# Hybrid layers of a 256-token block: heads side by side in the TensorE array, retention values centred first, mask and maximum in one instruction, four first PSUM banks

## The chip, the cores and the metric

The kernel runs on one core of one Trainium2 chip. The metric is the device time of one execution in microseconds (us); lower is better. The engines named here are TensorE (PE, with its weight loads PEld), VectorE (DVE), ScalarE (ACT) and SyncE (SP), which issues the DMAs of the weights.

## What is computed

Two blocks follow each other on 256 tokens of width 1024, all in float32. The first block (feed-forward, a gated linear recurrence, dilated attention) is not touched. The second puts 16 meta tokens in front (272 tokens) and runs two hybrid layers; each is a mixer and a feed-forward part. The change is in the mixer alone:

```python
q_r, k_r, v_r, g_r, u_p, q_f, k_f, v_f, f_logit = split(h @ w_in)
# retention, 4 heads, dk 48, dv 96
scores = einsum('bnihd,bnjhd->bnhij', rotary(q_r), rotary(k_r) * dk**-0.5) * dmask
inner  = einsum('bnhij,bnjhe->bnihe', scores, v_r)          # and the carried state
o_r = silu(g_r) * head_group_norm(o_r, ret_gn_g)            # (o - mean) * rsqrt(var + eps) * g, per head
# pooling, 4 windows
o_p = multiscale_pool(u_p, pool_w, pool_scale)
# forgetting attention, 6 heads of 64
c = cumsum(log_sigmoid(f_logit + b_f))
s = q_f @ k_f.T * d**-0.5 + c[:, None] - c[None, :]         # causal mask, softmax
o_f = softmax(where(mask, s, -1e30)) @ v_f
mix = concat([o_r, o_p, o_f]) @ w_out                       # then residual and layer norm
```

The mean over a head's 96 outputs is linear in the values: with values whose mean over the 96 entries is taken off first, the outputs have mean zero, because the mixing weights of a token are the same for all 96 entries.

## The kernel before, in words

Activations lie feature-major in SBUF: 8 tiles of 128 features by 272 (or 256) tokens. Every weight matrix comes in chunks of 128 output columns. A chunk is loaded by SP into one of four `raw` slots; ACT rounds it to fp32r (`whi`, L1047) and DVE subtracts to get the rest (`wlo`, L1522). PE multiplies with three fp32r products per 128x128 tile (L490 to L492), so that a chunk of the mixer's input projection is 24 matmuls of 272 columns. PE's work on a chunk is called a tile s here; ACT then copies its accumulator (L1384, semaphore `acc_free`) to where it is used.

`hybrid(l)` exists once for each engine, with a loop over the 22 tiles `s` of `MIX_ORDER` (gate 0, four for rotary q and k, three retention values, then keys, queries and values of the attention, two for the pool, three gates). What stands under `if s == n` is an order written out by hand: on PE it comes behind tile n, on ACT between the rounding of chunk s + 2 and the copy of tile s, on DVE behind the rest of chunk s + 2. Each engine's queue is in order, so what waits holds up all behind it. The two first tiles run together (`first_chunks`), as the features of x arrive.

Around the tiles lie the small products, in plain fp32, each of which appears as two matmul records: `ret_scores` (L881, two calls of two heads, each head in its own 32 rows of the array), `ret_values` (L853), `ret_means` (L896, all-ones by the outputs), `ret_variance` (L906), `ret_spread` (L913, the reciprocal deviation to all rows), `fox_scores` (per head: q by k over 64 rows, L830, and the cumulated logits over 12 rows by fp32r, L833, three token tiles), `fox_transposed` (L846), `fox_values` (L853, one head) and `pool_products` (L922). Tiles alternate between banks 0 and 1 (`two_banks`), so tile s waits until ACT has copied tile s - 2. All `fox_scores` use banks 2 and 3, and head h waits until DVE has read head h - 1.

On ACT, tile 0 is copied behind three instructions on the forget logits (L1366 to L1368, with a table load). On DVE stand the logarithm of the forget gates in eight parts (`cumulative_logits`), `rotate` (L1952 to L1954), `decay` (L1986), `centre` (L1994), `mask_max` (mask L1922, maximum L1927, three token tiles each), `normalise` (L1934, L1938) and the pool. Behind the tiles, PE begins the two first chunks of the output projection (`begin`, in `BEGIN_ORDER`) as their inputs become ready.

Of the kernel before, what the change touches and what calls it, by code (L numbers as in the profile page):

```python
# [73 lines left out]
BEGIN_ORDER = (6, 4, 5, 7, 0, 1, 2)  # L74
# [15 lines left out]
B_SEL = B_EXP + RET_HEADS * P  # L90
# [6 lines left out]
B_HEAD = B_CNT + 2 * TOK  # L97
B_LO = B_HEAD + RET_HEADS * RET_HEADS
# [32 lines left out]
def build(nc, x_in, meta_in, par_in, con_in, bias_in, con2_in, poolw_in, weights, out):  # L131
# [89 lines left out]
    rden_f = place("rden_f", [2, 3])  # L221
    assert cursor[0] <= hhi_at
# [106 lines left out]
    fx_done = sem("fx_done")  # L329
    fe_done = sem("fe_done")  # L330
# [4 lines left out]
    rot_done = sem("rot_done")  # L335
    up_zero = sem("up_zero")
# [8 lines left out]
    ret_mean = sem("ret_mean")  # L345
    ret_xc = sem("ret_xc")
# [72 lines left out]
    spread_bank = (6, 7, 6, 7)  # L419
# [66 lines left out]
    def _(pe):  # L486
# [310 lines left out]
        def hybrid(l):  # L797
# [15 lines left out]
            def fox_scores(h):  # L813

                rows = slice(HD * (h % 2), HD * (h % 2 + 1))
                pe.wait_ge(acc_free, mix_evicted(st, "q", h // 2))
                if h == 0:
                    pe.wait_ge(c_done, l + 1)
                    pe.wait_ge(sel_done, l + 1)
                    pe.wait_ge(vt2_copied, 2 * l + 1)  # L820
                if h == 2:

                    pe.wait_ge(vt2_copied, 2 * l + 2)
                if h:
                    pe.wait_ge(biased, HEADS + f0 + h)
                b = 2
                for q, (bank, c) in enumerate(((b, 0), (b, FOX_AT[1]), (b + 1, 0))):
                    n = FOX_COLS[q]
                    o = ps[0:QT[q], bank, c:c + n]
                    nc.tensor.matmul(o, qf[rows, h // 2, token_tiles(q)], kf[rows, h // 2, 0:n], start=True, stop=False)  # L830

                    parts = slice(LOGIT_ROW, LOGIT_ROW + LOGIT_ROWS)
                    last = nc.tensor.matmul(o, sel_r[parts, h * P:h * P + QT[q]], c_parts[parts, 0:n], start=False, stop=True)  # L833
                last.then_inc(scored, 1)

            def fox_transposed(h):
                pe.wait_ge(probs_ready, HEADS + f0 + h + 1)
                if h == 0:

                    pe.wait_ge(ret_xc, RET_HEADS * l + 1)  # L840
# [16 lines left out]
            def fox_values(h):  # L857
                o = ps[HD * (h % 2):HD * (h % 2 + 1), 5, :]
                pe.wait_ge(vt2_copied, 2 * l + 2)
                pe.wait_ge(pT_copied, HEADS + f0 + h + 1)  # L860

                pe.wait_ge(at_ready, PAIRS + 3 * l + h // 2)
                by_values(o, vf_tok, slice(HD * h, HD * (h + 1)), pT_fox[:, h % 2, :]).then_inc(pv_done, 1)
# [8 lines left out]
            def ret_scores(pair):  # L872

                if pair[0] == 0:
                    pe.wait_ge(rot_done, 4 * (l + 1))
                for k in range(3):
                    for half in range(2):
                        for h in pair:
                            rows = slice(32 * h, 32 * h + 32)
                            o = ps[0:QT[k], score_bank[h], KEY_AT[k]:KEY_AT[k] + KEY_COLS[k]]  # L880
# [5 lines left out]
            def ret_values(h):  # L886
                pe.wait_ge(vt2_copied, 2 * l + 1)
# [5 lines left out]
            def ret_means(h):  # L893

                pe.wait_ge(ret_osb, RET_HEADS * l + h + 1)
                nc.tensor.matmul(ps[0:RET_DV, out_bank[h], 0:TOK], ones_head[0:RET_DV, 0:RET_DV], osb[0:RET_DV, h, :],  # L896
                                 start=True, stop=True).then_inc(ret_mean, 1)

            def ret_variance(h):

# [25 lines left out]
            for s in range(WIN_TILES):  # L926
# [21 lines left out]
                if s == 12:  # L948
                    fox_scores(1)
# [1327 lines left out]
```

## Time and profile before

| | before |
|---|---|
| median of 3 runs | 1849.24 us (1844.86 to 1849.54) |
| profiled execution, its own time | 1849.01 us |
| its span in the profile | 1847.2 us |
| busy PE, PEld | 1801.1 us, 1623.2 us |
| busy DVE, ACT | 1298.9 us, 980.4 us |
| chain that ended last | PE 92%, DVE 5%, ACT 2% |

The spans of the engines overlap. A line of the profile names the source line (L), the engine, the operation, the tiles written and read, shapes and times. The PE spans of neighbouring matmuls overlap too, since they are pipelined: what one costs is the step to the next one's start. Layer 0 of the mixer (`mix0`) starts near 1128 us, layer 1 (`mix1`) near 1495 us.

### The profile page before, as it was taken

The numbers are of one execution on the slowest core, as the hardware profiler recorded it, in microseconds if no ns is written. First come the engines' busy times: TensorE is split into PE (matmuls) and PEld (weight loads), VectorE is DVE, ScalarE is ACT, GpSimd is POOL, SyncE is SP. The second block draws the span as 40 slices with busy tenths as digits, with TensorE's granted clock in tenths as the row PEclk, the third lists the DMA queues.
The fourth block names the chain that finished last, engine by engine and source line by source line (L and its number), as shares of the span: only waits on it lengthen the run. The fifth ranks groups of instructions, "written<-read, shape, count | busy, mean of one in ns | idle before, by whom it ended". The sixth has DMA issues, their size and how long they took to land.

```text
span 1847.2 us, 33301 instructions
## 1 busy us (share of the span) xinstructions
PE 1801.1 (98%) x11784; PEld 1623.2 (88%) x11784; DVE 1298.9 (70%) x2113; ACT 980.4 (53%) x1712; POOL 0.2 (0%) x4
## 2 busy tenths in 40 slices
PE   8999998999999999999899997999999989999998
PEld 7888998888898888888788887879999988788887
DVE  6776889777656776688877667568656575687765
ACT  5564695655456563555565545354434354556553
POOL 0000000000000000000000000000000000000000
PEclk9999999999999999999899998999999999999999
DMA  6565364556545565333455651323556433245562
GB/s 225 186 204 190 126 191 153 171 188 219 167 144 176 189 207 176 107 103 104 167 172 192 214 170 51 106 96 106 171 170 205 159 104 103 89 136 185 183 210 86
DMA packets 76637, 290.97 MB, mean 158 GB/s; under 512 B 9344, under 2 KB 11648, under 8 KB 76544
## 3 DMA queue, kind: packets, MB, share of 16 engines
q1 hardware_dynamic: 76544, 289.70, 48.2%
q8 instruction: 62, 1.02, 0.2%
q14 instruction: 31, 0.25, 0.0%
HBM read 288.62 MB, written 1.05 MB: 157 GB/s over the span
## 4 chain that ended last, share of the span: by engine, by line
PE 92%; DVE 5%; ACT 2%; issue 1%; DMA 0%; SPq 0%; ACTq 0%; DVEq 0%
PE psum L498 32%; PE psum L499 16%; PE psum L490 12%; PE psum L492 11%; PE psum L491 11%; PE psum L853 1%; PE psum L736 1%; PE psum L630 1%; DVE r L1694 1%; DVE wlo L1522 1%; PE psum L830 1%; PE psum L625 1%; PE psum L735 1%; PE psum L846 1%; PE psum L833 0%
## 5 line engine op out<-in xcount | busy, mean ns | idle before, releaser
L1522 DVE TENSOR_TENSOR wlo<-raw,whi 128x1024 fp32r<-128x1024 f32 (+3 forms) x496 | 644.7, 1309 | 268.6 <-ACT whi L1047 267.9
L498 PE MATMUL psum<-x_split,whi 128*128 128x512 f32 x1760 | 618.5, 395 | 6.4 <-DVE x_split L1557 3.8
L1047 ACT ACTIVATE whi<-raw 128x1024 fp32r<-128x1024 f32 (+3 forms) x496 | 548.8, 1119 | 39.0 <-PE psum L492 20.4
L499 PE MATMUL psum<-x_split,wlo 128*128 128x256 f32 x1760 | 494.2, 281 | 0.0
L498 PEld LDWEIGHTS psum<-x_split,whi 128*128 128x128 f32 x1760 | 331.0, 188 | 85.2 <-issue 3.9
L490 PE MATMUL psum<-x_split,whi 128*128 128x272 f32 (+1 forms) x1184 | 351.2, 297 | 13.7 <-ACT gsb L1384 7.7
L492 PE MATMUL psum<-x_split,wlo 128*128 128x272 f32 (+1 forms) x1184 | 342.1, 289 | 0.0
L491 PE MATMUL psum<-x_split,whi 128*128 128x272 f32 (+1 forms) x1184 | 341.5, 288 | 0.0
L499 PEld LDWEIGHTS psum<-x_split,wlo 128*128 128x128 f32 x1760 | 331.4, 188 | 0.0
L498 PE MATMUL psum<-h_split,whi 128*128 128x512 f32 x770 | 272.2, 397 | 0.0
L490 PEld LDWEIGHTS psum<-x_split,whi 128*128 128x128 f32 x1184 | 227.3, 192 | 22.5 <-ACT gsb L1384 8.2
L491 PEld LDWEIGHTS psum<-x_split,whi 128*128 128x128 f32 x1184 | 227.4, 192 | 0.2
L492 PEld LDWEIGHTS psum<-x_split,wlo 128*128 128x128 f32 x1184 | 227.2, 192 | 0.0
L499 PE MATMUL psum<-h_split,wlo 128*128 128x256 f32 x770 | 216.2, 281 | 0.0
L1115 ACT ACTIVATE small<-psum 128x256 f32<-128x256 f32 x220 | 84.4, 383 | 223.8 <-PE psum L499 223.6
L490 PE MATMUL psum<-h_split,whi 128*128 128x256 f32 (+3 forms) x614 | 178.2, 290 | 4.9 <-DVE wlo L1522 2.5
L492 PE MATMUL psum<-h_split,wlo 128*128 128x256 f32 (+3 forms) x614 | 175.4, 286 | 0.0
L491 PE MATMUL psum<-h_split,whi 128*128 128x256 f32 (+3 forms) x614 | 175.2, 285 | 0.0
L498 PEld LDWEIGHTS psum<-h_split,whi 128*128 128x128 f32 x770 | 144.7, 188 | 34.1
L1150 ACT ACTIVATE sq<-r 128x256 f32<-128x256 f32 (+2 forms) x70 | 29.4, 420 | 227.9 <-DVE r L1671 227.9
L499 PEld LDWEIGHTS psum<-h_split,wlo 128*128 128x128 f32 x770 | 145.6, 189 | 0.1
L1596 DVE TENSOR_TENSOR whole<-psum,small 128x256 f32<-128x256 f32 x220 | 93.1, 423 | 62.9 <-ACT small L1115 62.9
(229 smaller groups left out, 1820.8 us busy)
## 6 DMA issues: line engine op xcount, KB each, us to landing
raw<-w_in SPq DMA_DIRECT2D x264, 512.0 KB, 3.4
raw<-w_out SPq DMA_DIRECT2D x96, 704.0 KB, 4.1
raw<-w_mix SPq DMA_DIRECT2D x44, 512.0 KB, 3.4
raw<-w_rg SPq DMA_DIRECT2D x25, 512.0 KB, 3.8
raw<-w_q SPq DMA_DIRECT2D x24, 512.0 KB, 3.5
raw<-w_mixo SPq DMA_DIRECT2D x16, 576.0 KB, 3.7
raw<-w_kv SPq DMA_DIRECT2D x16, 512.0 KB, 4.3
raw<-w_rg_out SPq DMA_DIRECT2D x8, 640.0 KB, 3.9
```

The costliest lines, as they stand in the source:

```text
L490: nc.tensor.matmul(acc(bank, T), whi[slot][0:rows, w], hi, start=start, stop=False)
L491: nc.tensor.matmul(acc(bank, T), whi[slot][0:rows, w], lo, start=False, stop=False)
L492: return nc.tensor.matmul(acc(bank, T), wlo[slot][0:rows, w], hi, start=False, stop=stop)
L498: nc.tensor.matmul(ps[:, bank, :], whi[slot][:, w], split, start=start, stop=False)
L499: return nc.tensor.matmul(part(bank, 0), wlo[slot][:, w], split[:, 0], start=False, stop=stop)
L625: return nc.tensor.matmul(acc(4, T), ones_d, tile[:, t], start=first, stop=last)
L630: ins = nc.tensor.matmul(ps[:, 5, col + m:col + m + 1], tile[:, c:c + P], ones_d[:, 0:1], start=not started, stop=last and m == len(starts ...
L1047: nc.scalar.activation(whi[slot][:, 0:cols], raw[slot][:, 0:cols], ACT.Copy).then_inc(w_hi_done, count)
L1115: nc.scalar.activation(small[:, b, j % 2, :], part(j, 1), ACT.Copy).then_inc(small_out, 1)
L1150: nc.scalar.activation(sq[:, i + j, t], r[:, i + j, t], ACT.Square).then_inc(sq_done, 1)
L1522: V.tensor_tensor(wlo[slot][:, 0:cols], raw[slot][:, 0:cols], f(whi[slot][:, 0:cols]), ALU.subtract).then_inc(w_lo_done, 1)
L1596: ins = V.tensor_tensor(whole[:, b, j % 2, :], part(j, 0), small[:, b, j % 2, :], ALU.add)
```

## The change

1. Tiles 0 to 3 have a bank each (`mix_bank`); tiles 2 and 3 wait for no copy, tiles 4 and 5 for those of tiles 0 and 1 (wait s - 3), later ones as before. The three ACT instructions on the logits move to s = 2 (`forget_logits`) and read the copied gate.
2. `ret_scores` does four heads at once behind tile 6, in banks 4 to 7.
3. The transposed retention values are centred by DVE (`centre_values`: three sums, three scalar_tensor_tensor with a broadcast) as they leave PSUM, in place of three ACT copies. `ret_means` and `centre` are gone. ACT copies and squares each output from PSUM; `ret_values` run together behind tile 10.
4. `ret_variance` puts four heads in four groups of 32 columns of the array, the root and the reciprocal run over 128 rows, and `ret_spread` reads one row, through bank 5, one head behind the other.
5. `fox_scores` and `fox_values` work on pairs of heads: scores on row groups 0 to 63 and 64 to 127 with banks 2, 3 and 6, 7, logits now over 64 rows with zeros (a second copy of `c_parts` and `sel_r` in the other half), values on column groups 0 to 63 and 64 to 127.
6. `mask_max` is one `tensor_tensor_reduce` per token tile: (score + mask) * -1 and its minimum; `exps` scales by -1. `normalise` takes one reciprocal in place of three.
7. The orders on all three engines and `BEGIN_ORDER` are new.

```diff
+BEGIN_ORDER = (6, 7, 4, 5, 0, 1, 2)
+RET_ORDER = (2, 3, 0, 1)
...
+    mix_bank = lambda s: s if s < 4 else s % 2
...
-                    from_x(st, s // SLOTS, s % SLOTS, two_banks(s), st.u0 + s - 1)
+                    from_x(st, s // SLOTS, s % SLOTS, mix_bank(s), st.u0 + max(0, s - (3 if s < 6 else 1)))
...
+                for q in range(3):
+                    for h in heads:
+                        rows = slice(HD * (h % 2), HD * (h % 2 + 1))
+                        nc.tensor.matmul(out(h, q), qf[rows, pair, token_tiles(q)], kf[rows, pair, 0:FOX_COLS[q]],
+                                         start=q != 1, stop=False, skip_group_check=True)
+
+                for q in range(3):
+                    for h in heads:
+                        rows = slice(HD * (h % 2), HD * (h % 2 + 1))
+                        ins = nc.tensor.matmul(out(h, q), sel_r[rows, h * P:h * P + QT[q]], c_parts[rows, 0:FOX_COLS[q]],
+                                               start=False, stop=True, skip_group_check=True)
...
+                for k in range(3):
+                    for h in heads:
+                        e = h % 2
+                        ins = nc.tensor.matmul(ps[HD * e:HD * (e + 1), 5, QT_AT[k]:TOK], vf_tok[0:QT[k], k, HD * h:HD * (h + 1)],
...
+                for h in range(RET_HEADS):
+                    ins = nc.tensor.matmul(ps[32 * h:32 * h + 32, 5, 0:TOK], ones_head[0:RET_DV, 0:32], sqh[0:RET_DV, h, :],
+                                           start=True, stop=True, skip_group_check=True)
...
             for s in range(WIN_TILES):
                 tile(s)
                 if s == 6:
+                    ret_scores()
...
                 if s == 10:
+                    for h in RET_ORDER:
+                        ret_values(h)
+                if s == 11:
                     fox_scores(0)
                 if s == 12:
+                    ret_variance()
+                if s == 13:
...
+                    transposes(vf, 3, ((2, 0), (3, 0), (4, 0))).then_inc(vt2_done, 1)
+                if s == 14:
+                    ret_spread(0)
+                if s == 15:
+                    fox_transposed(0)
                     fox_scores(1)
...
+                if s == 2:
+                    forget_logits()
...
+                if s == 13:
+                    act.wait_ge(ret_var, l + 1)
+                    nc.scalar.activation(std4[:, :], ps[:, 5, 0:TOK], ACT.Sqrt, bias=eps[:, 0:1]).then_inc(ret_std, 1)
                     exps(0)
...
+                    ins = V.tensor_tensor_reduce(s_fox[0:m, h % 3, c:c + n], ps[0:m, at[0], at[1]:at[1] + n],
+                                                 con2[0:m, B_MASK + c:B_MASK + c + n], -1.0, 3e38, ALU.add, ALU.min,
+                                                 nmax_f[0:m, b, q:q + 1])
...
                 if s == 2:
+                    V.memset(f(c_parts[:, :]), 0.0)
+                    V.memset(den_f[:, :, :], 1.0).then_inc(den_one, 1)
                     cumulative_logits(0)
...
                 if s == 14:
+                    dve.wait_ge(ret_std, l + 1)
+                    V.reciprocal(std4[:, :], std4[:, :]).then_inc(ret_rstd, 1)
+                    normalise(0)
```

On DVE, s = 3 to 8 stay as they were: `rotate(0)` and part 1 of the logits at s = 3, parts 2 and 3 at 4, `rotate(1)` at 5, parts 4 and 5 at 6, `decay` at 7 and 8.

## Rows read from the trace of the kernel before

**Rows 1.** The page's first part: busy time of the engines over the span.
```profile
PE 1801.1 (98%) x11784; PEld 1623.2 (88%) x11784; DVE 1298.9 (70%) x2113; ACT 980.4 (53%) x1712; POOL 0.2 (0%) x4
```
**Rows 2.** Timeline of PE: start, us, instruction, idle before it; starts of both layers.
```profile
1138.24 0.59 PE L490 MATMUL psum<-x_split,whi 128*128 128x272 f32 x1 [3.87 <-ACT gsb L1384]
...
1158.32 0.39 PE L490 MATMUL psum<-x_split,whi 128*128 128x272 f32 x1
...
1506.46 0.60 PE L490 MATMUL psum<-x_split,whi 128*128 128x272 f32 x1 [3.88 <-ACT gsb L1384]
...
1525.22 0.39 PE L490 MATMUL psum<-x_split,whi 128*128 128x272 f32 x1
```
**Rows 3.** Timeline of ACT in that wait of layer 0.
```profile
1134.10 1.06 ACT L1047 ACTIVATE whi<-raw 128x1024 fp32r<-128x1024 f32 x1 [1.41 <-PE psum L492]
...
1136.05 1.28 ACT L1368 ACT_TABLE_LOAD   x1
1137.35 0.42 ACT L1368 ACTIVATE sgate<-sgate 12x272 f32<-12x272 f32 x1
```
**Rows 4.** Busy time by stretch: PE, PEld, DVE, ACT, POOL, PEclk, DMA, GB/s.
```profile
1138.22:1141.61 3.39, 3.37 (x15) 3.37 (x16) 2.24 (x3) 3.39 (x7) 0.00 (x0) 0.50 0.29 114
...
1137.59:1144.41 6.82, 6.17 (x27) 6.17 (x28) 3.37 (x3) 4.30 (x11) 0.00 (x0) 0.50 0.49 151
...
1574.49:1577.91 3.42, 3.42 (x16) 3.42 (x16) 3.30 (x7) 0.00 (x0) 0.00 (x0) 0.50 0.52 172
280.84:287.67 6.83, 4.36 (x21) 4.10 (x20) 6.52 (x9) 2.35 (x3) 0.00 (x0) 0.50 0.27 89
```
**Rows 5.** Timeline of PE in the recurrence stage, ahead of the last stretch of rows 4.
```profile
279.58 0.36 PE L490 MATMUL psum<-h_split,whi 128*128 128x256 f32 x1 [2.04 <-DVE h_split L1784]
```
**Rows 6.** The chain of waits in order of time, layer 0: start, us, what.
```profile
1156.37 2.02 PE psum L881 x24
...
1161.61 2.02 PE psum L881 x24
...
1178.58 1.09 PE psum L896 x4
...
1181.65 0.27 PE psum L833
...
1196.08 1.93 PE psum L906 x8
...
1213.88 1.13 PE psum L853 x6
```
**Rows 7.** PE's groups by shape: count, busy us, mean ns of one, both layers.
```profile
L881 PE MATMUL psum<-rot 32*112 32x272 f32 x32 | 4.7, 410 | 0.0
...
L896 PE MATMUL psum<-osb,con 96*96 96x272 f32 x16 | 4.5, 402 | 0.0
```
**Rows 8.** Timeline of DVE in layer 0, tiles 2 to 6.
```profile
1140.56 0.30 DVE L1540 TENSOR_SCALAR prod<-sgate 12x272 f32<-12x272 f32 x1
...
1144.59 0.44 DVE L1952 TENSOR_TENSOR rtmp<-rot_in,con 128x272 f32<-128x272 f32 x1 [1.85 <-ACT rot_in L1384]
...
1148.78 1.23 DVE L1522 TENSOR_TENSOR wlo<-raw,whi 128x1024 fp32r<-128x1024 f32 x1 [0.33 <-ACT whi L1047]
...
1155.68 1.22 DVE L1522 TENSOR_TENSOR wlo<-raw,whi 128x1024 fp32r<-128x1024 f32 x1
```
**Rows 9.** DVE's groups by shape: count, busy us, mean ns of one.
```profile
L1922 DVE TENSOR_TENSOR s_fox<-psum,con 64x272 f32<-64x272 f32 x12 | 5.1, 423 | 0.0
L1927 DVE TENSOR_REDUCE nmax_f<-s_fox 64x1 f32<-64x272 f32 x12 | 5.0, 418 | 0.0
...
L1541 DVE RECIPROCAL prod<-prod 12x272 f32<-12x272 f32 x2 | 3.7, 1848 | 0.1
```
**Rows 10.** Timeline of ACT around the root of the variance, layer 0.
```profile
1204.71 1.28 ACT L1452 ACT_TABLE_LOAD   x1
```
**Rows 11.** Busy time of the stretch in which ACT does one head's exponentials.
```profile
1216.57:1218.01 1.44, 1.44 (x9) 0.95 (x8) 0.71 (x3) 1.44 (x6) 0.00 (x0) 1.00 0.23 42
```

More of the change, by code:

```diff
@@ L221, in build @@
     rden_f = place("rden_f", [2, 3])
+    v_sum = place("v_sum", [3, RET_HEADS])
     assert cursor[0] <= hhi_at
@@ L806, in tile, with fox_scores @@
                 if s >= FIRST:
-                    from_x(st, s // SLOTS, s % SLOTS, two_banks(s), st.u0 + s - 1)
+                    from_x(st, s // SLOTS, s % SLOTS, mix_bank(s), st.u0 + max(0, s - (3 if s < 6 else 1)))
             def token_tiles(t):
                 return slice(QT_AT[t], QT_AT[t] + QT[t])
[L813 to L817, printed above, removed]
+            def fox_scores(pair):
+                heads = (2 * pair, 2 * pair + 1)
+                pe.wait_ge(acc_free, mix_evicted(st, "q", pair))
+                if pair == 0:
@@ L818, in fox_scores @@
                     pe.wait_ge(c_done, l + 1)
                     pe.wait_ge(sel_done, l + 1)
[L820 to L833, printed above, removed]
@@ L834, in fox_scores, with out @@
-                last.then_inc(scored, 1)
+                    pe.wait_ge(vr_centred, l + 1)
+                    pe.wait_ge(ret_sq, RET_HEADS * l + 2)
+                if pair == 1:
+                    pe.wait_ge(vt2_copied, l + 1)
+                if pair:
+                    pe.wait_ge(biased, HEADS + f0 + 2 * pair)
+                def out(h, q):
+                    bank = (2 if h % 2 == 0 else 6) + q // 2
+                    c = FOX_AT[1] if q == 1 else 0
+                    return ps[0:QT[q], bank, c:c + FOX_COLS[q]]
@@ L1479, in hybrid @@
             copy_transposed(5)
+            act.wait_ge(pool_mm, l + 1)
+            for m in range(2):
+                nc.scalar.activation(h_hi[:, RET_HEADS + m, :], acc(2 + m, TOK), ACT.Copy,
+                                     scale=par[:, C_PS + 2 * l + m:C_PS + 2 * l + m + 1]).then_inc(pool_hi, 1)
             next_chunk(by_name[f"mixo{l}"], 0, 0)
@@ L1932, in normalise @@
                 dve.wait_ge(probs, HEADS + f0 + h + 1)
-                for q in range(3):
-                    ins = V.reciprocal(rden_f[0:QT[q], b, q:q + 1], den_f[0:QT[q], b, q:q + 1])
-                link(ins)
+                link(V.reciprocal(rden_f[:, b, :], den_f[:, b, :]))
                 for q, (c, n, m) in enumerate(zip(FOX_AT, FOX_COLS, QT)):
@@ L1990, in hybrid, with centre_values @@
             hd = slice(0, RET_DV)
-            def centre(h):
-                dve.wait_ge(ret_mean, RET_HEADS * l + h + 1)
-                V.tensor_tensor(osb[hd, h, :], osb[hd, h, :], ps[hd, out_bank[h], 0:TOK], ALU.subtract).then_inc(ret_xc, 1)
+            def centre_values():
+                dve.wait_ge(vt2_done, 2 * l + 1)
+                by_head = lambda tile: tile.rearrange("p (h d) -> p h d", h=RET_HEADS)
+                for t in range(3):
+                    ins = V.tensor_reduce(v_sum[0:QT[t], t, :], by_head(ps[0:QT[t], 2 + t, 0:FOX_W]), AX.X, ALU.add, negate=True)
+                link(ins)
+                for t in range(3):
+                    n = QT[t]
+                    less = v_sum[0:n, t, :].unsqueeze(2).broadcast_to([n, RET_HEADS, RET_DV])
+                    ins = V.scalar_tensor_tensor(by_head(vr_tok[0:n, t, :]), less, 1.0 / RET_DV, by_head(ps[0:n, 2 + t, 0:FOX_W]),
+                                                 ALU.mult, ALU.add)
+                ins.then_inc(vr_centred, 1)
             def norm_output(h):
```

252 lines of the change are left out of this document (95 added, 157 removed).

## The prediction

> **What bounds the kernel now.** I read the page's first part, then the idle time of PE, then the granted clock by stretch, then the order of DVE and ACT where PE will arrive earlier. PE is busy for 98% of the span [rows 1], so time goes only where PE has fewer steps, waits less, or runs at the higher clock. In the two mixer stages three things are seen. First, PE stands still for 3.87 and 3.88 us when tile 2 wants bank 0 [rows 2]: ACT has the rounding of a chunk, two instructions on the logits, a table load of 1.28 us and an exponential ahead of the copy [rows 3]. Second, the granted clock is at 0.50 (1.2 GHz in place of 2.4) in five stretches of the two stages, of which rows 4 show the first, 6.82 us, and the last, 3.42 us; the first covers that wait, the last follows a run of small products. A stretch of 3.42 us that is full of work costs half of itself, 1.7 us. Third, a tile of 24 matmuls takes 3.2 us (from the end of one L881 group at 1158.39 to the next at 1161.61 [rows 6]), while the small products of a head cost up to 2.3 us.
>
> **Fewer steps on PE, for one layer.**
> - Scores of the retention: two calls of 2.02 us [rows 6] become one. Two heads in different row groups already run together: 32 matmuls of 272 columns keep PE busy for 4.7 us, where 16 with one head at a time need 4.5 us [rows 7]. I take 2.2 us for four heads; if only two overlap it stays at 4.0. Gain 1.8 (0 to 2.0).
> - Means: four matmul pairs, 1.09 us for two of them [rows 6]. Gain 2.0 (the second two start under the tail of a tile).
> - Scores of the attention: a head takes 2.25 us (from 1179.67, the end of L896, to 1181.92, the end of the last L833 [rows 6]), six heads 13.5 us. For a pair, q by k is two passes over 592 columns. The L881 group does two halves by two passes over 496 columns in 2.02 us, 1.02 ns per column and step; this gives 1.2 us for both heads together. The logits are one pass of 592 columns; a tile of 3.2 us for 24 times 272 columns is 0.49 ns per column, so 0.3 us together, 0.6 us one by one. With 0.3 us for filling the array twice it is 1.8 us, and 5.4 for three pairs. Gain 8.1. The worst end, no overlap at all, is 3.9 us a pair: gain 1.8.
> - Variance: 1.93 us [rows 6] for eight records, one head at a time. Four column groups of which each runs alone would stay there; together they are two steps of 0.27 and a fill, 0.75 us. Gain 1.2 (0 to 1.3).
> - Values of the attention: 1.13 us a head [rows 6], 6.8 us. No row shows two column groups at once. The nearest rows are the row groups of rows 7, which overlap fully; I take 1.2 us a pair, 3.6 us, gain 3.2, with 0 as the other end.
> - Spread: four single pairs in place of two double ones, 0.65 each against 0.54. Loss 0.4.
> - Transposes, retention values and pool stay.
>
> The sum is 1.8 + 2.0 + 8.1 + 1.2 + 3.2 - 0.4 = 15.9 us for a layer.
>
> On the column groups, the Trainium skill speaks in two ways. TensorE: Matmul & The Clock Gate, Part 3, has three column groups at 2.38 times the speed of one; by that a pair costs about 1.4 us and the sum loses 0.7 us. The same part says that weight loads go under running matmuls only where the row groups differ, and both heads of a pair use all rows here; by that nothing overlaps among columns (a rival below). In this trace loads do run under matmuls that use the same rows, since PE and PEld are busy for 98% and 88% of one span [rows 1].
>
> **The wait at tile 2, and what is late next.** Four banks take the 3.87 us away. PE then asks for tile 6 early, and tile 6 needs the rest of its chunk, which DVE does behind `cumulative_logits(0)`, `rotate(0)` and part 1. The first of them waits for the exponential of the logits. In the new order ACT does more ahead of that: a second rounding, five scaled copies of x and two tile copies. A stretch of 3.39 us holds one such rounding, five copies of x and one tile copy [rows 4]; with 0.3 for the other copy it is 3.7 us. Before, the exponential ended 3.67 us after the start at 1134.10 [rows 3], so now it ends 7.35 us after it. From there DVE needs 6.0 us to the rest of chunk 6 (1140.56 to 1148.78, less 1.85 and 0.33 idle [rows 8]), and 6.9 us more to the end of `rotate(1)` (1148.78 to 1155.68). So chunk 6 is ready 1.2 us later, 14.7 us after the start, where PE would be at 12.5 (four tiles of 3.13 and nothing else): a wait of 2.2 us. The rotation ends at 20.3 us; PE, with tile 6 done at 17.9, waits 2.4 us more. Four scores then take until 22.4 us. Tile 7 started 24.2 us after 1134.10 in layer 0 (1158.32), and in layer 1, counted from the same place before its wait, 22.9 us. The gain of the start is thus 1.8 us and 0.5 us, not 3.9 plus the clock: DVE's chain takes it over. Of the 15.9 us, 1.8 for the scores lie behind the second call at tile 7, which is simply gone (2.0), and the longer first call is counted here; the tail keeps 2.0 + 2.0 + 8.1 + 1.2 + 3.2 - 0.4 = 16.1.
>
> **A new wait at the first spread.** It stands behind tile 14 and needs the reciprocal of the deviation. On ACT, after the rounding behind tile 12: table load 1.28 [rows 10], root 0.4, table load 1.28 again for `exps(0)` of 1.44 [rows 11], a copy 0.3, a rounding 0.95, 5.6 us; ahead of these 1.5 us for a copy and a rounding; on DVE then the rest 1.1 and the reciprocal 1.85 [rows 9]. That is 10.1 us from the end of tile 12. PE needs 0.75 + 3.13 + 1.0 (transposes) + 3.13 = 8.0. A wait of 2.1 us, behind which tile 15 is queued. At the very end I find 0.8 us for the third pair's output, which is needed last. Centring, six instructions of some 0.5 us on DVE, hides beside tile 9 and 10; without cover it would cost up to 1.5 us. The tail's gain is 16.1 - 2.1 - 0.8 = 13.2 us per layer.
>
> **Mask and maximum.** Two instructions of 423 and 418 ns [rows 9] become one. It is no operation that the trace shows. One pass like the mask is the low end (1.1 us a head with three tiles), the sum of both the middle (1.8), the reciprocal, 1848 ns for 272 columns, the dearest row. I take 1.1 to 1.3; up to 1.8 costs nothing, since DVE has room in the tail. `normalise`, the memsets and the wider root and `sel_r` go with it at nothing, under PE's tiles.
>
> **Clock.** Two stretches in layer 0's tail and one in layer 1's go, 1.7 us each, if nothing takes their place. But a wait of 2.04 us [rows 5] in another stage was followed by 6.83 us at 0.50 [rows 4], and three waits of 2.1 to 2.4 us per layer are new. I charge one stretch of 3.4 us (1.7) at the start and one behind the spread for each layer, and one more for the two together: 8.5 us. Low end 0; high end 6.83 at each place, 17 us.
>
> **Sum.** Start 1.8 + 0.5, tails 26.4, old stretches 5.1, new ones -8.5: 25.3 us. From the profiled execution, 1849.0 us (0.2 below the median of the runs), this gives 1823.7, and I say 1824. Its own range is 1816 to 1832.
>
> **Rivals.**
> - Column groups, or heads with shared queues, don't overlap. Columns alone cost 2.5 us a layer (values back, of which the last wait swallows some), 1829; with no overlap for the attention's scores either, 2 x 8.7 us, 1841. For: the rule above. Against: rows 7. Chance 0.12, at 1829 to 1843.
> - The waits are longer, and each opens 6.83 us at half clock: some 12 us more, 1836. For: rows 4 and 5. Against: in the start DVE's chain decides anyway, so slow PE work there is half hidden. 0.14.
> - Slower: the new instruction costs as much as the reciprocal and some of a second pass, 2.0 us each, 6 us a head. DVE would then have 36 us of it beside some 25 us of other work from tile 12 on, where PE needs 50: laid out along the queues, the wait at the spread grows, since mask 1 stands ahead of the reciprocal, and each pair of scores waits for masks. At 4.0 us a head a layer loses 6 us, at 6 about 18: 1859. It decides from 5.1 us a head (1.7 us each). For: the operation is unseen. Against: no two-input row of that shape costs over 0.5 us. 0.06.
> - The change doesn't do what it says, because queues in order give back all of it: each of three waits doubles and no clock returns, 1845. 0.05.
> - Better: the waits stay under what lowers the clock, 1812 to 1816. 0.05.
>
> **Chances and range.** The forecast has 0.58. A run of this kernel can tell 0.3%, 5.5 us, from no change. Faster by more than that: 0.58 + 0.12 + 0.14 + 0.05 = 0.89; within: 0.05; slower: 0.06. The range that leaves out no more than 2 in 10 is 1815 to 1840.
>
> **What would show it.** L881 with 48 records in about 2.2 us; the score pair in 1.8; value pairs in 1.2; no wait of PE at tile 2, but some 2 us each at tile 6, ahead of L881 and at the first spread; mask and minimum near 0.45 us each. Wrong it would be if pairs start a full step apart, or if the clock is at 0.50 for more than 20 us of the two stages.

## The result and the profile after

The changed kernel takes 1826.01 us (median of four runs, 1824.91 to 1826.48), the kernel before 1847.62 us in the same series (1844.86 to 1849.54). The ratio is 0.9887 with a 95% interval of 0.9872 to 0.9902: 21.6 us faster. The profiled execution took 1825.73 us, its span is 1824.0 us, against 1849.0 and 1847.2 before. Forecast were 1824 and a gain of 25.3 us. One of the four executions of the kernel with the start in another order (below) took 6010.63 us and stands in no other number here.

In the changed kernel the lines have moved: L903 are the retention scores (L881 before), L839 and L845 the products and logits of the attention scores (with L833), L882 the attention values (L853), L919 the variance (L906), L927 the spread, L860 the transposes, L1906 mask and maximum (L1922 and L1927).

TensorE (PE) is as full as it was [rows 1], busy for 28.8 us less:

```profile
PE 1772.3 (97%) x11768; PEld 1607.0 (88%) x11768; DVE 1290.3 (71%) x2099; ACT 977.8 (54%) x1706; POOL 0.2 (0%) x4
```

The chain of waits of layer 0, in order of time: start, us, what. It shows how long each packed group is, in place of those of rows 6.

```profile
1153.95 2.12 PE psum L903 x48
...
1177.24 1.34 PE psum L839 x12
1178.58 0.49 PE psum L845 x6
...
1202.02 0.62 PE psum L927 x2
...
1216.22 1.14 PE psum L882 x12
```

Four retention heads take what two took in rows 6. A pair's attention scores take 1.34 + 0.49 us, where one head took 2.25. A pair's values take 1.14 us, where one head took 1.13 us. The variance, in the timeline of PE, has gone from 1.93 us to 0.67 (0.60 to the start of what follows):

```profile
1182.22 0.67 PE L919 MATMUL psum<-sqh,con 96*32 96x272 f32 x8
```

PE's waits, by line and releaser, first in the stretch of layer 0's mixer (from 1120 to 1260 us):

```profile
PE psum L492 <- DVE wlo L1505: 2.5, 1, 2.5
PE psum L927 <- DVE std L2044: 2.4, 1, 2.4
PE psum L588 <- DVE r L1654: 1.0, 1, 1.0
PE psum L903 <- DVE rot L1935: 0.8, 1, 0.8
PE psum L492 <- DVE h_split L1925: 0.8, 1, 0.8
```

Then in that of layer 1 (from 1465 to 1612 us), where the first two and the scores have the same lengths:

```profile
...
PE psum L588 <- DVE r L1654: 1.1, 1, 1.1
...
PE psum L492 <- DVE h_split L1925: 1.0, 1, 1.0
```

The wait for bank 0 at tile 2, 3.87 us in rows 2, is gone. In its place stand five waits, all for DVE: 2.46 us at tile 6, 0.80 ahead of the scores, 2.42 at the first spread, 0.79 and 1.01 at the end of the stage (0.75, 1.00 and 1.06 for the second, fourth and fifth in layer 1). They sum to 7.5 us in layer 0 and 7.7 in layer 1; the old wait was 3.9 in each.

The granted clock is at 0.50 (1.2 GHz) in these stretches among others; the columns are those of rows 4:

```profile
1148.32:1151.73 3.41, 3.32 (x15) 3.35 (x16) 3.27 (x7) 0.00 (x0) 0.00 (x0) 0.50 0.49 154
1192.69:1199.52 6.83, 6.83 (x28) 5.93 (x27) 3.08 (x10) 0.56 (x2) 0.00 (x0) 0.50 0.38 128
1595.46:1602.29 6.83, 6.63 (x29) 6.48 (x30) 4.12 (x9) 1.89 (x3) 0.00 (x0) 0.50 0.53 160
1547.68:1551.09 3.41, 3.41 (x17) 3.41 (x17) 2.22 (x7) 0.00 (x0) 0.00 (x0) 0.50 0.42 126
```

Each of the four begins between 0.2 us before and 1.0 us behind the end of a wait: of tile 6 at 1148.41, of the spread at 1192.53 and 1546.65, of the last one in layer 1 at 1595.66. A fifth, 3.41 us from 1503.30, stands at tile 6 of layer 1. PE is nearly full in them (busy for 3.32 to 3.41 of 3.41 us, 6.63 and 6.83 of 6.83), and a stretch costs half of its length where nothing else is waited for. The five sum to 23.9 us; in the kernel before the five of the same stages were 20.5.

By place the gain of 23.2 us in the span is, measured in PE's timeline from one sum over a row of ones (L627, L625 before) to the next (L588, L586 before): 144.3 to 131.4 us in layer 0, a gain of 12.9; 132.9 to 120.9 us in layer 1, 12.0; from there to the following sum 21.4 to 24.4 us, a loss of 3.0, in which the stretch at 1595.46 us lies; and 1.3 us in places that the change doesn't touch.

VectorE's (DVE's) groups by shape in layer 0's mixer (from 1130 to 1250 us), with count, busy us and mean ns, show the operation that no row of before held. It reads its result out in a second record:

```profile
L1906 DVE CUSTOM_DVE_ANT_0 s_fox<-psum,con 64x272 f32<-64x272 f32 x6 | 2.6, 428 | 0.0
L1906 DVE CUSTOM_DVE_ANT_0 s_fox<-psum,con 96x208 f32<-96x208 f32 x6 | 2.2, 364 | 0.0
...
L1906 DVE CUSTOM_DVE_ANT_0 s_fox<-psum,con 112x112 f32<-112x112 f32 x6 | 1.6, 262 | 0.0
...
L1906 DVE DVE_READ_ACCUMULATOR2_ANT nmax_f<- 112x1 f32 x6 | 0.5, 79 | 0.0
```

One pass costs what the mask alone cost [rows 9], and the read 0.08 us.

### The profile page after: what moved, and what is told of

It reads as the page before. It is cut to its first block, busy times and chain, and to the rows that moved or that the text cites. A ratio compares the mean times of both kernels' runs of the same rounds, so it can differ in the third digit from the quotient of the medians.

```text
span 1824.0 us, 33247 instructions
## 1 busy us (share of the span) xinstructions
PE 1772.3 (97%) x11768; PEld 1607.0 (88%) x11768; DVE 1290.3 (71%) x2099; ACT 977.8 (54%) x1706; POOL 0.2 (0%) x4
## 3 DMA queue, kind: packets, MB, share of 16 engines
q1 hardware_dynamic: 76544, 289.50, 50.2%
## 4 chain that ended last, share of the span: by engine, by line
PE 88%; DVE 7%; ACT 3%; issue 1%; DMA 0%; SPq 0%; ACTq 0%; DVEq 0%
PE psum L500 32%; PE psum L501 16%; PE psum L492 11%; PE psum L494 10%; PE psum L493 10%; DVE wlo L1505 2%; PE psum L738 1%; PE psum L632 1%; PE psum L627 1%; DVE r L1677 1%; PE psum L579 1%; PE psum L737 1%; ACT whi L1043 1%; PE psum L860 1%; PE psum L867 1%
## 5 line engine op out<-in xcount | busy, mean ns | idle before, releaser
L1043 ACT ACTIVATE whi<-raw 128x1024 fp32r<-128x1024 f32 (+3 forms) x496 | 548.8, 1119 | 43.0 <-PE psum L494 24.4
```

Source lines behind the costliest of these rows:

```text
L1043: nc.scalar.activation(whi[slot][:, 0:cols], raw[slot][:, 0:cols], ACT.Copy).then_inc(w_hi_done, count)
```

## The experiments

The kernel before was timed beside each series (1847.6, 1845.3, 1846.7 and 1846.6 us), so kernels of different series are compared by their ratios; one thousandth is 1.85 us. By the intervals of two ratios their difference is uncertain by some 4 us. The changed kernel stands at 0.9887.

**The four banks by themselves.** The kernel before, with the bank and waits of the change and with the exponential of the forget gate moved out of the first tile's copy:

```diff
+    mix_bank = lambda s: s if s < 4 else s % 2
...
-                    from_x(st, s // SLOTS, s % SLOTS, two_banks(s), st.u0 + s - 1)
+                    from_x(st, s // SLOTS, s % SLOTS, mix_bank(s), st.u0 + max(0, s - (3 if s < 6 else 1)))
...
+                if s == 2:
+                    forget_logits()
```

> The kernel before with the four first banks and the moved logits alone (part 1 of the change). Theory: DVE's chain takes the start over, because the exponential of the logits comes 3.7 us later: PE stands still about 2.2 us ahead of tile 6 and up to 2.4 us ahead of the first L881 group, and tile 7 starts only 1 to 2 us earlier in each layer; about 1845 us, 2 to 4 us under the kernel before. Rival: what is gained at tile 2 stays, 3.9 us of waiting and 1.7 to 3.4 us of half clock in each layer, 12 us under the kernel before, about 1836 us.

It took 1849.15 us, ratio 1.0021 (1.0008 to 1.0034): no gain, rather a loss of 4 us, not even the 2 to 4 us of the theory. PE's timeline shows why, start, us, idle before it:

```profile
1146.93 0.57 PE L491 MATMUL psum<-x_split,whi 128*128 128x272 f32 x1 [2.46 <-DVE wlo L1526]
...
1152.46 0.48 PE L882 MATMUL psum<-rot 32*112 32x272 f32 x2 [0.81 <-DVE rot L1958]
```

3.27 us of waits replace 3.87. In the profiled execution (1845.2 us, the second shortest of ten that lie from 1844.9 to 1855.7), layer 0 gains 1.6 us and layer 1 loses 1.0, the latter with three stretches of 3.41 us at half clock in the place of two. The rival, in which the whole wait and its clock are gained, falls. DVE's chain takes over, as the prediction said, and alone the banks are worth nothing that can be measured.

**The same products with the heads outermost.** The changed kernel, in which a head's pieces follow one another in the queue instead of alternating with those of the other head; products and places in the array are the same (the loops are those of the scores' products, of the logits and of the values):

```diff
-                for q in range(3):
-                    for h in heads:
+                for h in heads:
+                    for q in range(3):
...
-                for q in range(3):
-                    for h in heads:
+                for h in heads:
+                    for q in range(3):
...
-                for k in range(3):
-                    for h in heads:
+                for h in heads:
+                    for k in range(3):
```

> The changed kernel with the loop over the two heads put outside the loop over token tiles in fox_scores and fox_values; same matmuls, same tiles of the array, same banks. Theory: two heads overlap only when their matmuls stand next to each other in PE's queue; a pair of scores then takes 3.3 to 3.9 us in place of 1.83, a pair of values 2.2 in place of 1.15, together 7 to 9 us a layer, about 1840 to 1844 us. Rival: each group of rows or columns has its own order and overlap does not hang on neighbours: groups stay at 1.8 and 1.15 us, 1826 us.

1837.13 us, ratio 0.9946 (0.9930 to 0.9963), 10.9 us above the changed kernel by the ratios. PE's timeline, first of the changed kernel, then of this one:

```profile
1177.17 1.41 PE L839 MATMUL psum<-kf,qf 64*112 64x112 f32 x12
1178.51 0.56 PE L845 MATMUL psum<-c_parts,sel_r 64*112 64x112 f32 x6
...
1216.15 1.21 PE L882 MATMUL psum<-pT_fox,vf_tok 112*64 112x272 f32 x12
```

```profile
1177.54 2.72 PE L839 MATMUL psum<-kf,qf 64*112 64x112 f32 x12
1180.19 0.56 PE L845 MATMUL psum<-c_parts,sel_r 64*112 64x112 f32 x6
...
1220.44 2.33 PE L882 MATMUL psum<-pT_fox,vf_tok 112*64 112x272 f32 x12
```

The 12 records of a score pair and of a value pair take twice as long: these products are plain fp32, two records each, and now six records of one head stand in a row. For them the overlap hangs on the neighbour in the queue. The logits' 6 records don't move, although their loops are turned as well: these products are fp32r, one record each, with three of one head in a row. In both kernels they start in three pairs, one record of each head (4 ns apart in the changed kernel, 10 ns in this one), and take 0.49 and 0.50 us to the next start. So a neighbour in the queue is not needed for every kind of product; whether the kind or the number of records in a row decides, no run here tells.

From start to next start the score pair goes from 1.34 to 2.65 us and the value pair from 1.15 to 2.26. Three pairs of each in two layers are 14.5 us. The expected 14 to 18 came out as 11: the stretches at half clock sum to 50.2 us in place of 59.8, worth 4.8 us, while all waits of PE sum to 46.7 us against 45.3. The waits for the third pair's output (0.79 and 1.00 us) are swallowed, but those ahead of the retention scores are 1.7 us longer in the two layers.

**Mask and maximum as two instructions.** The changed kernel with the addition and the maximum apart again:

```diff
-                    ins = V.tensor_tensor_reduce(s_fox[0:m, h % 3, c:c + n], ps[0:m, at[0], at[1]:at[1] + n],
-                                                 con2[0:m, B_MASK + c:B_MASK + c + n], -1.0, 3e38, ALU.add, ALU.min,
-                                                 nmax_f[0:m, b, q:q + 1])
+                    ins = V.tensor_tensor(s_fox[0:m, h % 3, c:c + n], ps[0:m, at[0], at[1]:at[1] + n],
+                                          con2[0:m, B_MASK + c:B_MASK + c + n], ALU.add)
...
+                    ins = V.tensor_reduce(nmax_f[0:m, b, q:q + 1], s_fox[0:m, h % 3, c:c + n], AX.X, ALU.max, negate=True)
```

On ACT the scale of -1 of the exponentials goes with it.

> The changed kernel with mask and maximum as two instructions per token tile again. Theory: DVE gets 0.9 us more per head, 10.6 us in all, and PE's waits stay as they are since DVE has room there; within 1.5 us of 1826. Rival: the one instruction was what made room for the pairs; each pair of scores waits about 0.9 us, 4 to 6 us more, 1831 us.

The single run took 1832.4 us, 6.4 above the changed kernel, which by its number speaks for the rival. Its profile does not: the only new wait is 0.36 us in each layer, ahead of the first transposes of the third pair. PE's waits over 0.06 us sum to 49.3 us against 45.3, and only 0.7 of that are the masks: 3.0 stand ahead of the retention scores, 1.5 in each layer, where tile 6 ran at full clock and its half-clock stretch came behind the scores instead (told below). Three kernels below that keep the one instruction show the same in layer 0 (2.28 us ahead of the scores): the reciprocal first, the end in another order, the wait filled. Stretches at 0.50 sum to 66.6 us against 59.8, 3.4 us of time. That run alone couldn't settle it, so the question was put again where those are absent, below.

**The reciprocal first.** The changed kernel with DVE's reciprocal of the deviation ahead of the rest of chunk 16, which stands at s = 14:

```diff
+                if s == 14:
+                    dve.wait_ge(ret_std, l + 1)
+                    V.reciprocal(std4[:, :], std4[:, :]).then_inc(ret_rstd, 1)
                 rest(s)
...
                 if s == 14:
-                    dve.wait_ge(ret_std, l + 1)
-                    V.reciprocal(std4[:, :], std4[:, :]).then_inc(ret_rstd, 1)
                     normalise(0)
```

> The changed kernel with DVE's reciprocal of the deviation ahead of the rest of chunk 16 in its queue, nothing else. Theory: the wait of 2.4 us at the first spread is an order in DVE's queue (the reciprocal stands behind a chunk that ACT rounds only after the exponentials); it goes, and with it the stretch at half clock that follows (3.3 us in layer 0, 1.6 in layer 1): 8 to 10 us under the changed kernel, about 1817 us. Rival: the chunk's rest is late in its place and tile 16 or the first transpose waits; gain under 3 us, over 1823 us.

1816.92 us, ratio 0.9838 (0.9821 to 0.9854), as the theory had it. In the changed kernel DVE's timeline has

```profile
1189.49 1.23 DVE L1505 TENSOR_TENSOR wlo<-raw,whi 128x1024 fp32r<-128x1024 f32 x1 [3.72 <-ACT whi L1043]
1190.63 1.85 DVE L2044 RECIPROCAL std<-std 128x272 f32<-128x272 f32 x1
```

which shows DVE idle for 3.72 us, waiting for a rounding by ACT, then the rest of that chunk, then the reciprocal that PE stands for; ACT had ended the root by 1185.5 us, before most of that idle time. With the reciprocal first no wait is left at the spread in either layer, and neither of the two stretches at 0.50 behind it. The start of this trace has another thing to show: tile 6 at full clock, and a longer wait behind it.

```profile
1149.27 0.36 PE L492 MATMUL psum<-x_split,whi 128*128 128x272 f32 x1 [2.46 <-DVE wlo L1505]
...
1154.81 0.50 PE L903 MATMUL psum<-rot 32*112 32x272 f32 x4 [2.28 <-DVE rot L1935]
```

From tile 6 to the scores it is 5.54 us here, and 5.54 us in the changed kernel (1148.41 to 1153.95), where tile 6 ran at half clock and the wait was 0.80. DVE's chain decides, and a slow clock under it costs nothing.

**The start in another order.** The changed kernel with the forget gate's exponential one step earlier on ACT, ahead of the rounding at s = 1; on DVE the first part of the logits ahead of the rest at s = 1, the second rotation at s = 4 in place of 5, and the other parts of the logits behind both rotations:

```diff
-                round_ahead(st, s // SLOTS, s % SLOTS)
-                if s == 2:
+                if s == 1:
                     forget_logits()
+                round_ahead(st, s // SLOTS, s % SLOTS)
...
+                if s == 1:
+                    cumulative_logits(0)
                 rest(s)
...
                 if s == 3:
                     rotate(0)
+                if s == 4:
+                    rotate(1)
+                if s == 5:
                     cumulative_logits(1)
-                if s == 4:
+                if s == 6:
                     cumulative_logits(2)
                     cumulative_logits(3)
-                if s == 5:
-                    rotate(1)
...
```

> The changed kernel (1826.0) with VectorE's and ScalarE's work at the start of the layer in another order: the exponential of the forget logits ahead of the second tile's rounding, the sum of the logits ahead of the second tile's rest, the two rotations one tile earlier each, and the other sums after them. Nothing is added or left out. Theory (VectorE's chain, not the banks, sets the start now): the waits of 2.46 us at tile 6 and 0.80 and 0.75 us ahead of the retention scores shrink to under 0.5 us together, and so does the half-clock stretch of 3.41 us behind each (about 1 to 1.7 us lost in each): 2 x (2.9 + 1.3) = 8.4 us, 1817 to 1820. Rival (as with the four banks, something else is late next, ScalarE's gate or the wait for the running maximum's buffers): under 2 us gained, 1824 to 1826. Against both: the wait at the first spread (2.42 us) stays as it is in either case.

1811.38 us (1811.26 to 1814.10), ratio 0.9819 (0.9801 to 0.9837): 12.6 us below the changed kernel by the ratios, more than the 8.4 expected. Both waits of the start are gone in both layers. The three longest waits of PE in layer 1 are now

```profile
PE psum L927 <- DVE std L2045: 2.4, 1, 2.4
PE psum L588 <- DVE r L1654: 1.1, 1, 1.1
PE psum L492 <- DVE h_split L1925: 1.0, 1, 1.0
```

All waits of PE over 0.06 us, summed over the span, fall from 45.3 to 40.2 us; the stretches at 0.50 from 59.8 to 39.3, worth half of it, 10.3 us. The two give 15.3 us for a span that is 14.5 us shorter. More of the clock has come back than the stretches at the start: those at 510.0, 1267.78 and 1622.77 us are gone too and the one behind the first spread is halved, while two in other stages have doubled. The stretch that followed the last wait of layer 1 is gone as well, although that wait and the one before it stand there as before:

```profile
1583.00:1590.00 7.00, 6.17 (x50) 6.15 (x51) 5.94 (x13) 3.12 (x6) 0.00 (x0) 1.00 0.58 180
```

So those two waits by themselves don't lower the clock; the reading that tied the stretch at 1595.46 us to them alone is wrong.

**The end in another order.** The changed kernel with the third pair's output ahead of the rest of the first output tile, and the second tile's rest behind the first sum:

```diff
-            rest_of_chunk(*ahead(by_name[f"mixo{l}"], 0, 0))
             rest_of_output(2)
-            rest_of_chunk(*ahead(by_name[f"mixo{l}"], 0, 1))
-            add_to_ax(by_name[f"mixo{l}"])
+            rest_of_chunk(*ahead(by_name[f"mixo{l}"], 0, 0))
+            add_to_ax(by_name[f"mixo{l}"], ahead(by_name[f"mixo{l}"], 0, 1))
```

> The changed kernel with VectorE's order at the end of the stage turned: the third pair's output is split ahead of the first output tile's rest instead of behind it, and the second tile's rest comes behind the first sum. Theory (the two waits at the end, 0.79 and 1.00, 1.01 and 1.06 us, are one queue on VectorE, and the 6.83 us half-clock stretch at 1595.46 us hangs on them): both waits go in both layers, 3.9 us, and with them up to 3.4 us of clock: 1819 to 1823. Rival (the work is only moved: the first output tile's rest is then late for its own reader, and the wait turns up at the row of ones or at the next output tile): 1825 to 1828, with the waits' sum within 1 us of 3.9.

1821.21 us, ratio 0.9864 (0.9849 to 0.9879), 4.2 us below the changed kernel by the ratios. The time is in the theory's range, the waits say half of each: the first of the two is gone in both layers, the second stays, as the rival had it.

```profile
1242.45 0.47 PE L588 MATMUL psum<-r,con 128*128 128x272 f32 x1 [0.80 <-DVE r L1654]
...
1594.37 0.45 PE L588 MATMUL psum<-r,con 128*128 128x256 f32 x1 [1.06 <-DVE r L1654]
```

PE comes to L588 earlier by what it no longer waits, and DVE still has a rest of 1.35 us and a memset of 0.51 us ahead of the sum. The waits that are gone are 1.8 us, and in layer 0 the wait ahead of the scores is 1.5 us longer, at full clock of tile 6. Most of the gain is the clock: the stretches at 0.50 sum to 52.5 us against 59.8, and the 6.83 us at the end of layer 1 are gone although the wait of 1.06 us stands.

**The wait filled.** The changed kernel with four fp32 products that nobody reads ahead of the first spread (of 272 columns each, not of 112 as the expectation says):

```diff
+            def fill_wait():
+                pe.wait_ge(ret_std, l + 1)
+                for _ in range(4):
+                    nc.tensor.matmul(ps[:, 5, 0:TOK], ident, qf[:, 0, :], start=True, stop=True)
...
                 if s == 14:
+                    fill_wait()
                     ret_spread(0)
```

> The changed kernel with four fp32 matmuls of 112 columns that nobody reads put on TensorE between the end of the square root and the first spread, so that TensorE is at work in the part of the wait that remains; the reciprocal is still 1.85 us behind VectorE's other work, and the spread can't start earlier. Theory (the half-clock stretch of 6.83 and 3.41 us behind the wait of 2.42 us is TensorE's idleness, a cost of its own beside the wait): the wait plus filling stays at 2.4 us, the half-clock stretches at 1192.69 and 1547.68 us go: 3.4 + 1.7 = 5.1 us less, 1820 to 1822. Rival (the half-clock stretches are not tied to this wait): they stay or turn up elsewhere, 1825 to 1828.

1820.25 us, ratio 0.9860 (0.9845 to 0.9875). DVE releases the spread as late as before, and PE is at work or idle for 2.57 us ahead of it, against 2.42 idle. But the clock stays up behind it, and the kernel is 5.0 us shorter by the ratios:

```profile
1190.92 2.00 PE L926 MATMUL psum<-qf,con 128*128 128x272 f32 x8
...
1193.49 0.69 PE L932 MATMUL psum<-std,con 1*96 1x272 f32 x2 [0.58 <-DVE std L2050]
...
1193.60:1200.00 6.40, 6.40 (x51) 4.85 (x52) 4.33 (x11) 2.41 (x6) 0.00 (x0) 1.00 0.38 132
```

The third line is the busy time of the stretch behind it: 51 records in 6.4 us at 1.00, where the changed kernel had 28 in 6.83 us at 0.50. The same holds in layer 1. The two stretches behind the spreads were 10.2 us, 5.1 us of time. This is the clock's price apart from the wait's: the idleness of PE, not the spread's lateness, costs it. That the measured 5.0 us equal this price is in part chance, since the profile has more changes: stretches of another 8.4 us less outside the spreads, the 6.83 us at the end of layer 1 among them, and against that a wait ahead of layer 0's scores that is 1.5 us longer, and the filling itself.

**All three orders.** The edits of the reciprocal, the start and the end together.

> The changed kernel with the three orders of VectorE together: reciprocal first (as in e4, which measured 1816.9), the start as in e5, the end as in e6. Theory (the three waits are separate and each brings its own stretch of half clock): the gains add, 9 + 8 + 5 = 22 us, 1802 to 1808. Rival (the half-clock stretches are not removed but fall elsewhere, and only the waits' own 2 x (2.4 + 3.3 + 1.9) = 15 us add): 1811 to 1814.

1800.56 us (1798.5 to 1801.7), ratio 0.9751 (0.9737 to 0.9764), 25.1 us below the changed kernel and just under the expected 1802 to 1808; the three alone give 9.1 + 12.6 + 4.2 = 25.9. The gains add. In the stretch of layer 0's mixer one wait of the five is left, in layer 1 the same one:

```profile
PE psum L588 <- DVE r L1654: 0.8, 1, 0.8
```

All waits over 0.06 us sum to 30.0 us (45.3 in the changed kernel), the stretches at 0.50 to 39.6 (59.8): 15.3 + 10.1 = 25.4 us, and the span is 25.2 us shorter. This kernel is faster than the kernel before and than the changed one.

**Two banks under the three orders.** The last kernel with tiles in two banks from the first on:

```diff
-    mix_bank = lambda s: s if s < 4 else s % 2
+    mix_bank = lambda s: s % 2
...
-                    from_x(st, s // SLOTS, s % SLOTS, mix_bank(s), st.u0 + max(0, s - (3 if s < 6 else 1)))
+                    from_x(st, s // SLOTS, s % SLOTS, mix_bank(s), st.u0 + max(0, s - 1))
```

> The kernel with all three orders (1800.6) with only two first banks, as in the kernel before: tile 2 waits until the first tile is copied out, tile 3 until the second. Theory (the four banks do work once VectorE's chain is out of the way): in the trace with four banks ScalarE ends its copy of the first tile at 1134.2 us and of the second at 1139.1 us, and TensorE would want tile 3 at about 1138.1: a wait of about 1 us at tile 3 in each layer and, as the running chain is fed later, up to 1 us more of clock in each: 1802.5 to 1805. Rival (the banks were never the matter, only the order of the forget gate's exponential was): under 0.5 us in each layer, 1800 to 1801.5. A third: the whole old wait of 3.87 us comes back, with its clock, 2 x 5 us: 1811.

1807.28 us, ratio 0.9789 (0.9772 to 0.9805): 7.0 us dearer than with four banks, and above the expected 1802.5 to 1805. The rival without any effect falls, and so does the one with the whole old wait; the theory's mechanism is there, with a second wait that it had not counted, at tile 2, since ACT ends its copy at 1133.8 us only:

```profile
1133.84 0.39 PE L492 MATMUL psum<-x_split,whi 128*128 128x272 f32 x1 [1.12 <-ACT gsb L1374]
...
1138.73 0.39 PE L492 MATMUL psum<-x_split,whi 128*128 128x272 f32 x1 [1.61 <-ACT rot_in L1374]
```

2.7 us in each layer are 5.4 of the 7.0. The banks that were worth nothing by themselves are worth this once the order on ACT and DVE lets PE use them.

**Two mask instructions under the three orders.** The kernel with all three orders and the edit of the two masks.

> The kernel with all three orders (1800.6) with mask and maximum in two instructions again. In the run of the changed kernel with two instructions the time was 1832.4 (one run), 6.4 above, of which the waits at the third transposes explain 0.37 us in each layer and the half-clock stretches 3.4 us. Theory (one instruction spares VectorE 1 us or so a head, and little of it lies on the path): one wait of 0.4 us in each layer, 0.7 us in all, and up to 2 us of clock: 1801 to 1803.5. Rival (the fused instruction carries more of the gain than its own wait shows): the 6 us again, 1806 to 1808.

1801.68 us, ratio 0.9755 (0.9739 to 0.9771): 0.7 us by the ratios, 1.1 by the medians, no more than can be told from nothing. The wait is the one seen before, in each layer:

```profile
PE psum L860 <- DVE s_fox L1922: 0.4, 1, 0.4
```

So of the 6.4 us of the open run the fused instruction has 0.7 us of waits and 1 us or so of time. The rest goes, by that run's profile, with where the half clock fell, which no repetition of it tests.

## Why the prediction was right, step by step

The kernel came out 2 us above the forecast, inside its range; the mechanism held, and the sizes of several terms did not. That the sum came so near is in part luck, as told at the clock and the waits. No run takes back the four-head scores, the variance or the centring alone: their shares are read from the trace.

- **Fewer steps on PE.** Forecast 15.9 us a layer, measured 16.4: retention scores 2.05 us for the one call (forecast 2.2), score pair 1.83 (1.8: its products 1.34 against 1.2, its logits 0.49 against 0.3, and 0.3 forecast for filling the array), variance 0.60 to the next start (0.75), value pair 1.15 (1.2), spread 0.62 each (0.65); the means' 2.0 us are gone. The value pair was the unseen one. The experiment with the heads outermost gives 2.26 us for the same two heads, so the overlap in column groups is worth a factor of 1.97. It also shows a condition of the fp32 pairs that the prediction took for granted: the order in the queue. Its price, 14.5 us of products and 10.9 us of time, would have been half of the gain.
- **The rival of the column groups** falls. The Trainium skill's TensorE: Matmul & The Clock Gate, Part 3, gives three column groups 2.38 times one and says that weight loads overlap running matmuls only across row groups. Here two column groups that use the same rows reach 1.97 of 2 with a load for each product, so the rule does not decide the time of such pairs, and the measurement goes before it.
- **The start.** Forecast was that DVE's chain takes the four banks' gain over, with a wait of 2.2 us at tile 6 and 2.4 ahead of the scores. Measured 2.46, and 2.28 where tile 6 runs at full clock (0.80 where it doesn't, 5.54 us for both together either way). The gain of the start was forecast at 1.8 and 0.5 us; counted from the stage's first product to tile 7 in layer 0 it is 2.0 (30.4 to 28.4 us), and from the sum over the row of ones before in layer 1 it is 0.8 (36.2 to 35.4), of which 0.4 is a shorter wait at the head of the stage (1.03 to 0.67 us). The kernel with the four banks alone confirms it, and the new order of the start shows what stood behind the chain: 12.6 us.
- **The wait at the spread.** Forecast 2.1 us, measured 2.42 in both layers.
- **The centring** hid, as forecast: six instructions of 0.54 to 0.56 us on DVE, and PE waits for nothing between the scores and the first spread.
- **The end of the stage** is the term that was mis-sized. Forecast was one wait of 0.8 us. Measured are two, 0.79 + 1.01 and 1.00 + 1.06 us. The second, at the row of ones that takes the first sum, was not foreseen: DVE's queue there (the split, a rest of 1.34, a memset of 0.51, the sum) was not laid out past the third output. It costs 2.1 us in the two layers.
- **The clock.** The charge of 8.5 us came out right in sum and wrong in its terms. Of it 3.4 stood for the starts; stretches of 3.41 us did come there, and cost nothing, since the wait behind them shrank by as much. Behind the spreads were 6.83 and 3.41 us (5.1 us, charged 3.4), and at the end of layer 1 6.83 us (3.4, charged 1.7 for the two layers). 8.5 again, by other ways; that the sums agree is luck. Together with the two at the starts the clock was at 0.50 for 23.9 us of the two stages. The prediction had called more than 20 us a sign that it was wrong, and on the clock this sign came. The old stretches, 5.1 us in the tails, are indeed gone, but 3.41 us from 1622.77 and others outside the two stages came up.
- **Sum.** 2 x 16.4 us less work, less 2 x 3.7 us of more waiting, is 25.4 us. The span gained 23.2, so the clock took 2.2 net. The waits' sum, too, came out by errors that cancel: 7.5 us a layer were forecast, 7.5 and 7.7 measured, with 1.6 us less ahead of the scores and 1.0 and 1.3 more at the end.
- **Mask and maximum.** 0.43 + 0.36 + 0.26 us and three reads of 0.08 are 1.3 us of records a head, with overlaps 1.0. This is the low end of the bounds. The slower rival would have decided from 5.1 us a head, and falls. Nothing was forecast for it on the path; the two runs say 0.7 us of waits.
- **The rival of longer waits and 6.83 us of half clock each**, at 1836, did not come, but it was the nearest: two of the six places had 6.83 us.

What stays open is where a stretch at 0.50 falls. The filled wait shows that one idle spell brings one; the orders of the start and of the end show that the waits at the end of the stage came with one and without. No run here tells how much idleness is needed how close together.

## What to carry to other kernels

When PE's wait is taken away at a bank, list what the other engines still have queued ahead of what PE will ask for next: here the banks by themselves were worth nothing, the order of the start on DVE and ACT 12.6 us, and under all three orders (25 us) the banks were worth 7. Plain fp32 products of heads packed into row and column groups should alternate in the queue product by product; with the heads one after the other the same packing gave next to nothing (2.26 us for two heads' values against 1.13 for one). The fp32r logits, three records a head, overlapped in either order. An instruction that PE stands for goes ahead of work that only has to be done some time, and a wait of some 2 us has to be priced with the clock behind it.

## What the runs showed of the hardware

- Two plain fp32 products with the same rows of the array, up to 112, and 64 columns each in different column groups run together: 1.15 us for the twelve of a pair when they alternate, 2.26 when they don't. Four column groups of the variance bring 1.93 us down to 0.60, a factor of 3.2.
- The logits' fp32r products of two heads, over 64 rows each in different row groups, run together whether the heads alternate (0.49 us for six records) or stand three and three in the queue (0.50).
- Four fp32 products of 272 columns, eight records that keep PE busy for 2.00 us in a wait spared 6.83 and 3.41 us at 1.2 GHz behind it.
- The combined add and minimum costs 428 ns for 272 columns, as much as the plain addition of 423 [rows 9], and 75 to 79 ns for reading the minimum.
- A reciprocal of 128x3 takes 0.16 us in the mean, against 1.85 for 128x272 and 1.85 for 12x272 [rows 9]; it is the columns that cost.
